# Two joints of a three-layer transformer kernel in token halves, and four split weight panels instead of two

## The reference

```
h = rms_norm(x, pre);   mixed = mixer(h) @ w_out;   x = x + rms_norm(mixed, post)
h = rms_norm(x, pre2);  f = (silu(h @ gate) * (h @ up)) @ down;  x = x + rms_norm(f, post2)
```

## Time and profile before

| what | value |
|---|---|
| median of 3 runs | 2433.84 us (2431.91 to 2439.47) |
| the profiled execution's own time | 2432.14 us |
| its span, first to last instruction | 2429.8 us |
| TensorE matmul busy | 2329.2 us, 96% |
| ScalarE, VectorE, GpSimd busy | 877.9, 1016.1, 1004.8 us |
| mean granted TensorE clock | 0.978 of 2.4 GHz |
| DMA | 210 MB, 87 GB/s on average |

### The profile page before, as it was taken

One profiled execution on the slowest core, in us unless ns is written; L12 is line 12 of the kernel. 1 busy time (PEld: TensorE's weight loads), 2 busy tenths in 40 slices (PEclk: granted clock), 3 DMA queues, 4 the chain that ended last, 5 costly groups with the idle time before them and its releaser, 6 DMA issues.

```text
span 2429.8 us, 41306 instructions
## 1 busy us (share of the span) xinstructions
PE 2329.2 (96%) x17380; PEld 1913.5 (79%) x17380; DVE 1016.1 (42%) x1577; ACT 877.9 (36%) x1445; POOL 1004.8 (41%) x553
## 2 busy tenths in 40 slices
PE   7999999999899999999989999999999999999998
PEld 6867788888786778888867888686888777888886
DVE  6164522211465452221156987266343455322212
ACT  5174432222425442232243232635333244333222
POOL 4423544444542354444464444335000365444443
PEclk9999999999999999999999999989999899999999
DMA  6601333333431123333343333323000322333331
GB/s 172 150 17 53 98 102 96 94 95 98 106 99 36 37 77 96 97 100 91 98 118 91 97 100 107 100 74 114 4 4 4 140 71 80 93 98 101 91 96 66
DMA packets 386314, 210.30 MB, mean 87 GB/s; under 512 B 36928, under 2 KB 378664, under 8 KB 385876
## 3 DMA queue, kind: packets, MB, share of 16 engines
q1 hardware_dynamic: 383011, 196.78, 28.5%
q0 software_dynamic: 2448, 9.70, 1.0%
q10 hardware_dynamic: 672, 1.18, 0.1%
HBM read 196.75 MB, written 12.41 MB: 86 GB/s over the span
## 4 chain that ended last, share of the span: by engine, by line
PE 90%; DVE 3%; ACT 3%; issue 2%; POOL 2%; ACTq 0%; DMA 0%; POOLq 0%; DVEq 0%
PE ps L1958 24%; PE ps L1960 24%; PE ps L1959 24%; PE ps L2371 3%; PE ps L2358 2%; PE ps L2075 2%; PE ps L2336 2%; PE ps L2050 1%; PE ps L2060 1%; POOL x_res L750 1%; POOL w_lo L689 1%; PE ps L1917 1%; PE ps L2385 1%; PE ps L2038 1%; ACT w_hi L858 1%
## 5 line engine op out<-in xcount | busy, mean ns | idle before, releaser
L689 POOL TENSOR_TENSOR w_lo<-raw,w_hi 128x1024 fp32r<-128x1024 f32 (+2 forms) x344 | 811.2, 2359 | 947.7 <-ACT w_hi L858 943.9
L1958 PE MATMUL ps<-h_hi,w_hi 128*128 128x512 f32 x2016 | 802.3, 398 | 30.9 <-ACT h_hi L940 12.9
L1959 PE MATMUL ps<-h_hi,w_lo 128*128 128x512 f32 x2016 | 792.6, 393 | 0.0
L1960 PE MATMUL ps<-h_lo,w_hi 128*128 128x512 f32 x2016 | 792.3, 393 | 0.0
L858 ACT ACTIVATE w_hi<-raw 128x1024 fp32r<-128x1024 f32 (+2 forms) x344 | 356.9, 1038 | 1165.7 <-PE ps L1960 1160.6
L1958 PEld LDWEIGHTS ps<-h_hi,w_hi 128*128 128x128 f32 x2016 | 383.7, 190 | 126.4 <-issue 42.7
L1960 PEld LDWEIGHTS ps<-h_lo,w_hi 128*128 128x128 f32 x2016 | 383.3, 190 | 81.7
L1959 PEld LDWEIGHTS ps<-h_hi,w_lo 128*128 128x128 f32 x2016 | 384.1, 191 | 79.9 <-issue 1.6
L1958 PE MATMUL ps<-hid_hi,w_hi 128*128 128x512 f32 x528 | 205.4, 389 | 0.0
L1959 PE MATMUL ps<-hid_hi,w_lo 128*128 128x512 f32 x528 | 205.4, 389 | 0.0
L1960 PE MATMUL ps<-hid_lo,w_hi 128*128 128x512 f32 x528 | 205.4, 389 | 0.0
(11 more groups left out here) (328 smaller groups left out, 2654.1 us busy)
## 6 DMA issues: line engine op xcount, KB each, us to landing
raw<-in_w_gu SPq DMA_DIRECT2D x88, 512.0 KB, 3.8
raw<-in_w_in SPq DMA_DIRECT2D x56, 512.0 KB, 3.8
raw<-in_w_down SPq DMA_DIRECT2D x32, 448.0 KB, 3.7
raw<-in_ffn_w_gate SPq DMA_DIRECT2D x22, 512.0 KB, 3.8
raw<-in_ffn_w_up SPq DMA_DIRECT2D x22, 512.0 KB, 3.9
raw<-in_w_in_b SPq DMA_DIRECT2D x20, 512.0 KB, 4.4
raw<-in_w_down SPq DMA_DIRECT2D x16, 512.0 KB, 4.1
raw<-in_w_out SPq DMA_DIRECT2D x16, 512.0 KB, 4.0
```

Source lines behind the costliest of these rows:

```text
L689: nc.gpsimd.tensor_tensor(lo[:, k0:, :], src[:, k0:, :], hi[:, k0:, :].bitcast(f32), ALU.subtract).then_inc(lo_done, 1)
L1958: nc.tensor.matmul(bank, wh[:, k, :], ah[:, 0:width], start=first, stop=False)
L1959: nc.tensor.matmul(bank, wl[:, k, :], ah[:, 0:width], start=False, stop=False)
L1960: return nc.tensor.matmul(bank, wh[:, k, :], al[:, 0:width], start=False, stop=end)
```

## The change

**Halves.** For `out0` and `out2` the last two output groups, the norm behind them and the first pair of `gu0` or `gu2` are done for tokens 0 to 255 and then for tokens 256 to 511. TensorE's order becomes: group 6 and group 7 of half 0, groups 6 and 7 of half 1, the pair on half 0, the pair on half 1, all with 256-column matmuls. Inside lie the feature sums and spreads of each half, two columns or 256 columns each. The second spread goes to bank 7. The square of group 6 is no longer added on VectorE but summed by TensorE, as that of group 7. Every elementwise step of the joint is issued twice with 256 columns. The next linear's panels 0 and 1 and the last two of this one are held at once, which takes four buffers.

**Four split panels.** Outside layer 2 (`wide`) `w_hi` and `w_lo` have four buffers each and `raw` has three: the fourth `raw` slot is the memory of a `w_lo`. In these stretches ScalarE splits one panel further ahead. Only `lora` and `rwkv_out` keep the panels in pieces. `o_raw` and one `v_chunk` move to other memory, and ScalarE's last output of an attention waits for GpSimd's last but one.

In the diff, `add_residual_in_halves` is GpSimd's; of the three functions named `joint_in_halves` the first is ScalarE's, the second VectorE's, the third TensorE's.

```diff
+        for i in range(2):
+            w_hi.append(at(f"w_hi{2 + i}", [P, KD, P], spare + 8192 * i, f32r))
+            w_lo.append(at(f"w_lo{2 + i}", [P, KD, P], spare + 8192 * i + 4096, f32r))
...
+        HALF_SPLIT = ("lora", "rwkv_out")
+        in_halves = {L[name].p0 + 2: i + 1 for i, name in enumerate(HALF_SPLIT)}
+        def wide(p):
+            return p < lora.p0 - 6 or p >= L["out2"].p0 + 2
...
+        raw_slot = oldest_first(lambda p: (1, 2, 3) if wide(p) else (1, 2, 3, 0))
+        split_slot = oldest_first(lambda p: (0, 1, 2, 3) if wide(p) else (0, 1))
...
-                if p >= 4:
-                    sp.wait_ge(lo_done, p - 3)
+                if raw_before[p] is not None:
+                    sp.wait_ge(lo_done, raw_before[p] + 1)
...
+                if tile == 7:
+                    act.wait_ge(hl, parts_before(v0) + 7)
...
-            def groups(name):
+            def groups(name, count=None):
                 l = L[name]
-                for i in range(l.groups):
+                for i in range(count or l.groups):
                     last = l.p0 + (i + 1) * l.per_group
-                    split_hi(last + 1)
+                    more = 1 if wide(last + 2) and wide(l.p0) else 0
+                    split_hi(last + 1 + more)
                     act.wait_ge(used, last)
                     if not (name in BEFORE_NORM and i == l.groups - 1):
-                        split_hi(last + 2)
+                        split_hi(last + 2 + more)
                     yield i, (l.g0 + i) % 4
...
-                    if c == 6 and name in PAIRED:
-                        split_hi_half(name)
...
+            def add_residual_in_halves(name, src):
+                split_lo(L[name].p1 + 2)
+                for half in range(2):
+                    for c in range(0 if half else 1, KD):
+                        pool.wait_ge(sg["post_scaled"], scaled_before(name) + KD * half + c + 1)
+                        x = x_res[:, c, cols_of(half)]
+                        nc.gpsimd.tensor_tensor(x, x, src[:, c, cols_of(half)], ALU.add).then_inc(sg["x_new"], 1)
...
+            def joint_in_halves(name, dst, sq, gain, after):
+                for i, b in groups(name, l.groups - 2):
+                    nc.scalar.activation(sq[:, i, :], ps[:, b, :], ACT.Square).then_inc(sg["post_sq"], 1)
+                    nc.scalar.activation(dst[:, i, :], ps[:, b, :], ACT.Copy).then_inc(bank_free[b], 1)
+                nc.scalar.activation(eps[:, 7:8], eps[:, 0:1], ACT.Sqrt)
+                split_hi(l.p1 + 2)
...
+                out_of(l.groups - 2, 0)
+                out_of(l.groups - 1, 0)
+                std_of(0)
+                for c in range(KD):
+                    high_of(c, 0)
+                    if c == 0:
+                        out_of(l.groups - 2, 1)
+                    if c == 3:
+                        out_of(l.groups - 1, 1)
+                    if c == 5:
+                        std_of(1)
+                    if c >= 4:
+                        square_of(c - 4, cols_of(0))
+                for c in range(KD):
+                    high_of(c, 1)
+                    if c == 3:
+                        split_hi(L[after].p0 + 3)
+                    square_of(c, cols_of(1) if c < 4 else slice(0, TOK))
+                split_hi(L[after].p0 + 5)
+                std()
...
+            def joint_in_halves(post, version, late_gain):
+                sum_squares(sq, KD - 2)
+                rstd(2)
+                spread()
...
+                for c in range(KD + 2):
+                    if c < KD:
+                        scale(c, 0)
+                    if c == 0:
...
+                        nc.vector.tensor_tensor(x, x, src[:, 0, cols_of(0)], ALU.add).then_inc(sg["x_new"], 1)
+                    if c >= 2:
+                        low_of(c - 2, 0)
+                    if c == 6:
+                        rstd(NT, 2)
+                spread()
+                for c in range(KD + 2):
+                    if c < KD:
+                        scale(c, 1)
+                    if c >= 2:
+                        low_of(c - 2, 1)
...
+            def joint_in_halves(name, sq, after):
+                n["step"] += KD - 3
+                def sums(half, c):
+                    if c in tail:
+                        pe.wait_ge(sg["post_sq"], n["out"] + KD - 1 + 2 * half + c - tail[0])
+                    else:
+                        pe.wait_ge(sg["sum_step"], n["step"])
...
+                for half in range(2):
+                    for i in tail:
...
+                        for k in range(KD):
+                            if not half and i == tail[0] and k == 5:
+                                sums(0, 0)
+                            if half and i == tail[0] and k == 3:
+                                sums(0, tail[0])
+                                sums(0, tail[1])
+                            if half and i == tail[1] and k == 1:
+                                spread(0)
+                            last = three(l.g0 + i, p, k, operand(name, l, k, i, 0), cols_of(half), k == 0, k == KD - 1)
...
+                pair_start(after)
+                for half in range(2):
+                    for k in range(KD):
+                        for i in range(2):
+                            last = three(a.g0 + i, a.p0 + i, k, operand(after, a, k, i, 0, half), cols_of(half),
+                                         k == 0, k == KD - 1)
...
+                        if not half and k == 1:
+                            for c in (0, tail[0], tail[1]):
+                                sums(1, c)
+                        if not half and k == 4:
+                            spread(1)
```

More of the change, by code:

```diff
@@ L188, in build @@
         pT = at("pT", [P, PT_BUFFERS, SPAN_A], so + SCORE_BUFFERS * 1552)
-        o_raw = at("o_raw", [P, 2, TOK], spare + 2048)
+        o_raw = [at(f"o_raw{i}", [P, TOK], h_off + 16384 * i + 7 * 2048) for i in range(2)]
         rpb_raw = at("rpb_raw", [P, HEADS, 8, 32], so)
@@ L548, in build, with cols_of, parts_before, added_before @@
         conv_steps = [(c, s) for c0 in range(0, KD, 2) for s in range(TAPS) for c in (c0, c0 + 1)]
+        IN_HALVES = {"out0": 4, "out2": 12}
+        JOINTS = ("out0", "down0", "out1", "down1", "out2", "down2")
+        HALF = TOK // 2
+        def cols_of(half):
+            return slice(HALF * half, HALF * half + HALF)
+        def parts_before(version):
+            return sum(2 * KD if v in IN_HALVES.values() else KD for v in range(version))
+        def added_before(name):
+            return KD + scaled_before(name)
+        def scaled_before(name):
+            return sum(2 * KD if n in IN_HALVES else KD for n in JOINTS[:JOINTS.index(name)])
+        def tails_before(name):
+            return sum(2 for n in JOINTS[:JOINTS.index(name)] if n in IN_HALVES)
         BEFORE_NORM = ("out0", "down0", "out1", "down1", "out2", "down2")
+        def ahead_of_norm(name):
+            return 2 if name == "down1" else 3
         T_KK = KD
@@ L734, in attention @@
                 output(7)
-            added = [0]
             def add_residual(name, src):
@@ L1329, in spread, with sum_squares @@
                 dve.wait_ge(sg["spread_done"], n["spread"])
-            def sum_squares(sq):
-                for c in range(KD - 1):
+            def sum_squares(sq, count=KD - 1):
+                for c in range(count):
                     n["post"] += 1
@@ L1988, in project @@
                     pe.wait_ge(*gates_read)
-                for i in range(2 if name in PAIRED else 0, l.groups):
+                for i in range(2 if name in PAIRED else 0, l.groups - 2 if name in IN_HALVES else l.groups):
                     g = l.g0 + i
@@ L2007, in project @@
                                 pe.wait_ge(lo_done, p + 1)
-                            last = three(g, p, k, operand(name, l, k, i, q), width, q == 0 and k == 0,
+                            last = three(g, p, k, operand(name, l, k, i, q), slice(0, width), q == 0 and k == 0,
                                          q == l.per_group - 1 and k == pan.kc - 1)
@@ L2187, in _ @@
             project("out0")
-            residual(mix_sq)
-            ffn("0")
+            joint_in_halves("out0", mix_sq, "gu0")
+            ffn("0", begun=True)
             project_late("q1")
```

246 lines of the change are left out of this document (169 added, 77 removed).

## The result

The changed kernel takes 2439.51 us (median of 20 runs), the kernel before 2431.32 us in the 20 runs beside it: a ratio of 1.0029, 95% interval 1.0020 to 1.0038. The forecast was 2438.3, with "within 0.3%" as the likeliest class, so it holds, but near that class's upper edge: the loss is 7.0 us by the ratio and 8.2 by the medians, where I had worked out 4.5. One of the twenty runs took 9121 us, at a mean granted clock of 0.553, and is left out of the ratio. The profiled executions have spans of 2429.8 and 2437.3.

A forecast was written before the change was run, and what follows sets the result against it. TensorE, with matmuls filling 96% of the span, was taken as the bound. Two joints at +2.5 us each gave +5.0, q1 -0.5, so +4.5 on 2433.8: 2438.3 us, range 2425 to 2445.

The forecast's parts named there:

- the wait at the first sum: Tail, half 0: TensorE waits 2.6 us for VectorE's add, until T0 + 4.4; T0 is the start of out0's group 6.
- the clock step behind it: In the tail, after TensorE's wait for its first sum: 3.3 us at half speed, costing 1.6 us a joint.
- Rival A: No clock step, the rest as forecast: 2435.1 us; chance 0.25.
- tail and pair, half 0: TensorE's tail ends at 16.1 after T0, the pair starts without the 4.29 us pause, chunks come every 0.9 us.
- First wait in half 1: Pair, half 1: chunk 0 is ready at 25.3 after T0, and TensorE waits 1.4 us for it.
- the buffers: Four split panels, three raw slots: -0.5 us at q1, 0 at gu1, no weight waits behind the joints.
- the end of the pair: Half 1: chunk 7 at 32.8, pair ends at 33.6 after T0; GpSimd's lo of panel 2 holds TensorE 0.1.
- q1: Four split panels save the 0.61 us piece between h_hi 6 and 7, after which TensorE waited 0.34: -0.5 us.
- what there was to win: 11.0 us in each of two joints: 8.1 between last matmul and pair, 2.9 lost to the half clock.
- rival C: h_lo and add exclude each other whole, period 1.14 us; +9.9 us, 2443.7; chance 0.16.

The follow-up runs named there:

- The filled wait: The changed kernel with four 512-column matmuls into an unread bank ahead of the first sum: 2440.31 us, ratio 1.0031.
- The filled whole joint: The kernel before, whole joints, with matmuls into an unread bank in TensorE's idle places of its six residual joints: 2432.29 us, ratio 0.9997.
- the two filled kernels: Unread matmuls in the kernel before's joints: 2432.29 us; in the changed kernel with first sum later, panel 2 split early, whole joints and half-0 pair start filled: 2428.68 us.
- the late sum alone: The changed kernel with the first sum moved from the first tail group to the second, on half 0: 2436.57 us, ratio 1.0014.
- the last kernel: The changed kernel with later first sum, GpSimd's lo parts held until VectorE's last h_lo of half 1, panel 2's lo part in two pieces: 2428.61 us, ratio 0.9987.
- the first group: Changed kernel with whole joints (2432.36 us), halves at out0 alone (2436.60), first sum later (2436.57), or wait filled with matmuls (2440.31); kernel before beside them 2431.46.

## Why the prediction was right, and where it was off

**Right: the wait at the first sum.** Forecast 2.6 us, sums begun at T0 + 4.4; measured 2.33 and T0 + 4.3, in both joints, for the add and the lo part that the earlier trace rows had shown. The rows of the old trace were enough to see it.

**Right: the clock step behind it.** Forecast 3.3 us at half speed for 1.6; measured 3.4 at 0.53, for 1.5 (16 matmuls of 0.213 us where 0.120 is the pitch). The filled wait shows that it hangs on the pause. Rival A, no such step, is out.

**Right: tail and pair, half 0.** Pair start forecast at 16.1 + 1.6 = 17.7, measured 17.6; no pause; 0.88 us per chunk against 0.9. First wait in half 1: 0.91 us where I had 1.4.

**Right: the buffers.** No loss shown by them, and no weight waits behind the joints of the changed kernel.

**Luck: the absolute time.** The forecast of 2438.3 lies 1.2 us from the 2439.5 measured, but it stood on 2433.8, the median of three runs, and twenty gave 2431.3. The loss itself was forecast as 4.5 and came as 7 to 8.

**Off, the term that was mis-sized: the end of the pair.** I let VectorE's chunk 7 come at 32.8 and GpSimd's lo of panel 2 hold TensorE 0.1. I did ask what the lo part holds up on TensorE, and not what it holds up on VectorE, though the earlier trace rows had just shown it. Measured: an h_lo of 2.08 us, a wait of 1.56, a first pre-sum of 2.88 and a wait of 0.66 for it. The pair ended 0.6 us later than forecast with the clock step, and panel 2 and the pre-sums came another 0.8 later: 3.8 instead of 2.5 at out0. At out2 the wait of 1.57 also drew a half clock, and it was 4.6.

**Off: q1.** Forecast -0.5 for the piece of 0.61 us that goes. The last h_hi came 19.3 us after the sums' start where it had been 19.5 (640.84 - 621.55 and 636.82 - 617.37), and TensorE's last wait is still 0.34: ScalarE waits 0.26 us for GpSimd's add at that chunk instead. I had costed the cover away but not asked what stood next.

**Off: what there was to win.** I wrote that 2.9 us are lost to the half clock and that 11.0 us a joint are there to be won. The filled whole joint of out0 shows 0.5 us for the clock. While GpSimd feeds a chunk each 1.65 us, a TensorE that needs 1.36 at full clock only waits instead. This did not touch the forecast's sum, which was made against the joint's measured end, but it led my expectations of the two filled kernels wrong, by 12 us and by 6.

**The shared port pair.** The rows: the add 0.69 us alone and 2.46 beside a lo part of 2.35 that started 0.43 us earlier, an add of x 0.42 and 2.56, h_lo 0.49 and 2.08. The Trainium skill (SBUF — State Buffer, section "SBUF: two separate sides") says that of a VectorE instruction with two SBUF inputs and a GpSimd instruction that reads SBUF, the one that starts first keeps the port pair for its whole length and the other is blocked: the trace agrees for every one of these, the VectorE instructions ending 0.3 to 0.5 us after GpSimd's. It does not fit the chain of half 0 as closely. There GpSimd's adds, 0.73 us at their shortest, and h_lo, 0.48 at its shortest, run at 0.88 a chunk, not at the 1.2 of their sum. So rival C, whose period of 1.14 was worked out from that sum, did not come, and yet its rule set the two largest waits. The price of the rule is the length of GpSimd's instruction, so it is high only beside the long ones.

## What to carry to other kernels

Before halving a stage to start it earlier, follow the chain that feeds it: its length in halves against its length whole, and the earliest moment at which the first half can be handed over. One full-width sum placed too early in TensorE's queue took back the whole lead. And look at what GpSimd runs beside each short VectorE instruction on the path. Moving the sum and GpSimd's long lo parts took nine us off the changed kernel, more than the halves win over the kernel before at their best (2.7).

## What the runs showed of the hardware that was not expected

- A half clock of 10 us right behind a pause cost 0.5 us at out0. TensorE at 1.2 GHz was slower than its feed (2.56 us a chunk against 1.70), but at full clock it was faster (1.36), and the five and a half chunks left were enough to make up the rest. In the tail, where TensorE set the pace, 3.4 us of it cost 1.5.
- Whether a pause of 1.5 to 2.3 us was followed by a half clock differed between joints of the same execution with the same pause (1.56 and 1.57 us, at out0 none, at out2 3.4 us of it), and it was 6.9 us long behind two such pauses. The runs spread from 2426.7 to 2438.3 with the late sum alone and from 2426.4 to 2431.7 in the last kernel; that the pauses cause the spread is not shown, since the kernel before went from 2427.9 to 2445.7 beside the first group.
- Two instructions that start within 0.05 us of each other decided 2.8 us of a joint: with the halves at out0 alone, GpSimd's last add of x was short (0.73), two h_lo were held and the pair ended at T0 + 38.6; in the changed kernel the add was stretched (1.02), one was held and it ended at 35.8.
